# Gated linear layer: the scores' diagonal as elementwise products of keys and queries, summed over the features on TensorE by a column of ones

## What is computed

```
b = cumsum(g);  decay[t,s,d] = exp(b[t,d] - b[s,d]) for s <= t, else 0
A[t,s] = sum_d q[t,d] * k[s,d] * decay[t,s,d]
o[t]   = sum_s A[t,s] * v[s]  +  (q[t] * exp(b[t])) @ S
S      = exp(b_last) * S + sum_s k[s] * exp(b_last - b[s]) * v[s]^T
```

## Time and profile before

| | us |
|---|---|
| median of 3 runs | 1822.11 (1821.92 to 1822.14) |
| the profiled execution's own time | 1821.95 |
| its span, first to last instruction | 1820.2 |
| TensorE (PE) busy | 1803.8, 99% |
| weight loads (PEld) busy | 1518.1, 83% |
| VectorE (DVE) busy | 1270.2, 70% |
| ScalarE (ACT) busy | 942.4, 52% |
| HBM traffic | 179 GB/s mean |

### The profile page before, as it was taken

How to read it: one execution, slowest core, us unless ns; L and a number is a source line. 1 busy time by engine, 2 the same in 40 slices (tenths; PEclk the granted TensorE clock), 3 DMA queues, 4 the chain that set the end, 5 groups by cost and what they waited for, 6 DMA issues and landing times.

```text
span 1820.2 us, 24366 instructions
## 1 busy us (share of the span) xinstructions
PE 1803.8 (99%) x8863; PEld 1518.1 (83%) x8863; DVE 1270.2 (70%) x1720; ACT 942.4 (52%) x1310; POOL 37.8 (2%) x116
## 2 busy tenths in 40 slices
PE   8999999999999999999999999999999999999999
PEld 7899998778888888887888888888878888888887
DVE  6766766588556755767887878787777556577764
ACT  4555554455465545636554545454445444565542
POOL 2000000000000004000000000000000000000000
PEclk9999999999999999999999999999999999999999
DMA  8555454668789887575554555544767776555443
GB/s 294 173 175 151 138 174 152 204 182 188 179 153 214 178 178 167 197 240 153 177 174 152 168 173 153 181 151 158 226 181 235 211 219 208 161 162 162 160 166 114
DMA packets 175067, 326.72 MB, mean 179 GB/s; under 512 B 16824, under 2 KB 24912, under 8 KB 174208
## 3 DMA queue, kind: packets, MB, share of 16 engines
q1 hardware_dynamic: 173840, 321.04, 61.2%
q10 hardware_dynamic: 576, 4.19, 0.6%
q0 software_dynamic: 560, 0.26, 0.1%
HBM read 319.68 MB, written 5.77 MB: 179 GB/s over the span
## 4 chain that ended last, share of the span: by engine, by line
PE 96%; DVE 2%; ACT 1%; issue 1%; DMA 0%; DVEq 0%
PE acc L388 27%; PE acc L390 27%; PE acc L389 27%; PE ps L650 2%; PE ps L2889 2%; PE ps L498 1%; PE acc L355 1%; PE acc L354 1%; PE acc L353 1%; ACT wsp L304 1%; PE ps L683 1%; DVE wsp L324 1%; PE acc L371 0%; PE acc L377 0%; PE acc L375 0%
## 5 line engine op out<-in xcount | busy, mean ns | idle before, releaser
L324 DVE TENSOR_TENSOR wsp<-wraw,wsp 128x1024 fp32r<-128x1024 f32 x576 | 696.3, 1224 | 333.1 <-ACT wsp L304 330.5
L304 ACT ACTIVATE wsp<-wraw 128x1024 fp32r<-128x1024 f32 x576 | 597.3, 1053 | 361.4 <-PE acc L390 329.1
L388 PE MATMUL acc<-wsp,ta 128*128 128x512 f32 x1664 | 660.3, 397 | 6.0 <-DVE wsp L324 3.8
L390 PE MATMUL acc<-wsp,ta 128*128 128x512 f32 x1664 | 649.8, 391 | 0.0
L389 PE MATMUL acc<-wsp,ta 128*128 128x512 f32 x1664 | 648.4, 390 | 0.0
L388 PEld LDWEIGHTS acc<-wsp,ta 128*128 128x128 f32 x1664 | 312.8, 188 | 72.9 <-issue 4.9
L390 PEld LDWEIGHTS acc<-wsp,ta 128*128 128x128 f32 x1664 | 312.4, 188 | 66.6
L389 PEld LDWEIGHTS acc<-wsp,ta 128*128 128x128 f32 x1664 | 313.0, 188 | 62.0
L388 PE MATMUL acc<-wsp,tb_hi 128*128 128x512 f32 x576 | 228.4, 397 | 0.0
L390 PE MATMUL acc<-wsp,tb_lo 128*128 128x512 f32 x576 | 225.1, 391 | 0.0
L389 PE MATMUL acc<-wsp,tb_hi 128*128 128x512 f32 x576 | 224.6, 390 | 0.0
(11 more groups left out here) (332 smaller groups left out, 1584.8 us busy)
## 6 DMA issues: line engine op xcount, KB each, us to landing
wraw<-in_ml_w_in SPq DMA_DIRECT2D x129, 512.0 KB, 5.9
wraw<-in_a_w_in SPq DMA_DIRECT2D x128, 512.0 KB, 3.8
wraw<-in_kv_w SPq DMA_DIRECT2D x64, 512.0 KB, 3.9
wraw<-in_b_w_in SPq DMA_DIRECT2D x64, 512.0 KB, 4.4
wraw<-in_mla_w_in SPq DMA_DIRECT2D x49, 512.0 KB, 4.5
wraw<-in_mla_w_out SPq DMA_DIRECT2D x32, 512.0 KB, 4.0
wraw<-in_ml_w_out SPq DMA_DIRECT2D x32, 512.0 KB, 4.4
wraw<-in_a_w_out SPq DMA_DIRECT2D x32, 512.0 KB, 3.9
```

The lines of the kernel that those rows point to most:

```text
L304: nc.scalar.activation(unit_of(whi, n, SPLIT, w), unit_of(wraw, n, RAW, w), ACT.Copy).then_inc(w_high, 1)
L324: nc.vector.tensor_tensor(unit_of(wlo, n, SPLIT, w), unit_of(wraw, n, RAW, w), unit_of(whi, n, SPLIT, w).bitcast(F32), ALU.subtract).then_ ...
L388: nc.tensor.matmul(o, xh, wh, start=first, stop=False)
L390: m = nc.tensor.matmul(o, xl, wh, start=False, stop=end)
```

## The change

On VectorE, the masking of the 8 whole squares leaves step 24. In its place `diag` does `scale(0)` at once, and then two elementwise products of all keys by all queries, [128 features x 512] each, into room 1 of `kx` and of `qx`; `distance(2)` follows. On TensorE, `diag` moves from after unit 21 to after unit 22 and waits for those two products. It has again 8 fp32 matmuls, with a 128 x 128 block of products as the stationary operand and one column of ones as the moving one, so that 8 columns of PSUM bank 0 get the sums over features. VectorE then makes `aT` at step 25, as the identity times the sum of each row, in one instruction over [128 x 1024].

```diff
-        L2_AT = {"turn": 16, "decay": 17, "diag": 21, "level": [23, 25, 27, 29, 31, 33, 35, 37], "gate": 38, "pv": 39,
+        L2_AT = {"turn": 16, "decay": 17, "diag": 21, "sums": 22, "level": [23, 25, 27, 29, 31, 33, 35, 37], "gate": 38, "pv": 39,
...
                     distance(0)
                     distance(1)
-                    dve.wait_ge(l2["dg"], 1 + g)
-                    nc.vector.tensor_tensor(aT, ps2(0).rearrange("p (n t) -> p n t", t=P),
-                                            ident[:].unsqueeze(1).to_broadcast([P, 8,
-                                                                                P]), ALU.mult).then_inc(l2["at"], 1)
                     scale(0)
+                    for half, room in enumerate((kx, qx)):
+                        n = slice(half * 2 * T, (half + 1) * 2 * T)
+                        nc.vector.tensor_tensor(room[:, 1, :], flat(kT2)[:, n], flat(qT2)[:, n],
+                                                ALU.mult).then_inc(l2["dg"], 1)
                     distance(2)
+
+                def diagonal():
+
+                    dve.wait_ge(l2["dg"], 3 + 3 * g)
+                    nc.vector.tensor_tensor(aT, ident[:].unsqueeze(1).to_broadcast([P, 8, P]),
+                                            ps[:, 0, 0:8].unsqueeze(2).to_broadcast([P, 8, P]), ALU.mult).then_inc(l2["at"], 1)
...
                 if u == L2_AT["diag"] + LAG:
                     diag()
+                if u == L2_AT["sums"] + LAG:
+                    diagonal()
...
                 def diag():
-                    pe.wait_ge(l2["qT"], 1 + g)
-                    pe.wait_ge(l2["kt"], 1 + g)
+                    pe.wait_ge(l2["dg"], 2 + 3 * g)
                     for n in range(8):
-                        m = nc.tensor.matmul(ps2(0)[:, n * P:(n + 1) * P], kT2[:, n, :], qT2[:, n, :], start=True,
-                                             stop=True)
+                        products_of = (kx, qx)[n // 4][:, 1, n % 4 * P:(n % 4 + 1) * P]
+                        m = nc.tensor.matmul(ps[:, 0, n:n + 1], products_of, ones[:, 0:1], start=True, stop=True)
                     m.then_inc(l2["dg"], 1)
...
-                if u == L2_AT["diag"]:
+                if u == L2_AT["sums"]:
                     diag()
```

## The result

The changed kernel takes 1845.74 us (median of 4 runs, 1844.88 to 1846.59) against 1822.11 before: 1.0129 times as long, 95% interval 1.0117 to 1.0141, some 23.6 us more. The forecast was 1835.2 with a range of 1830 to 1842: right in the sign, but the time lies 3.7 us above the range. The profiled execution took 1844.88, with a span of 1843.2, 23.0 more than before.

What follows compares the result with a forecast made beforehand. The prediction took the length of TensorE's queue (busy 99% of the span) as the bound: block gain nothing, waits 4 x 3.3 = 13.2 us, all else nothing, added to 1821.95 gives 1835.1, stated as 1835.2; range 1830.0 to 1842.0.

Steps and rivals of the forecast that it cites:

- TensorE's block itself: TensorE's 16 records per group: paced by weight loads, 16 x 0.107 = 1.71 us as before, a gain of nothing.
- When the products are there: TensorE after unit 22: waits from 900.63 until VectorE's second product ends at 903.8, some 3.2 us per group.
- the sum of 4 x 3.3: Unit 23 on TensorE starts 3.3 us later, start-up included, in each of four groups: 13.2 us.
- What else moves: Other work on VectorE, ScalarE, DMA queues and later TensorE steps: no further wait, nothing given back, 0 us.
- none felt: Rival, TensorE behind unit 22: VectorE has the products by the time TensorE comes; 1822, or 1819 with cheap records; chance 0.03.
- a second one: Rival: products come later than added up, by a further ScalarE wait or late level 1; 4.5 us more, 1839.7; chance 0.04.
- The pause slows TensorE down: Rival, TensorE behind each pause: a slow stretch costing 1.8 us more each, 7.3 in all, 1842.5; chance 0.22.

Runs made afterwards that it cites:

- e1: The changed kernel with the two products moved to the head of VectorE's step 24, ahead of the first distance; 1822.15 us, ratio 0.9999.
- e2: The kernel before the change, with the moving operand of the diagonal's 8 products cut from 128 columns to 1; 1822.10 us, ratio 0.9999.
- e7: e1 with the products rounded to fp32r and two rounded columns of ones, one weight load per matmul instead of two; 1820.78 us, ratio 0.9992.
- e5: The changed kernel with the two products placed between distance(1) and scale(0), so that TensorE's pause is shorter; 1835.42 us, ratio 1.0074.
- e6: The changed kernel with TensorE's block one unit later, after unit 23 instead of 22; 1825.22 us, ratio 1.0018.
- e3: The changed kernel with 7 filling matmuls (identity by 256 columns of ones) on TensorE ahead of its wait for the products; 1837.15 us, ratio 1.0083.
- e4: The changed kernel with the old 128-column block in the new place, behind the wait for the two products, computed but not used; 1842.10 us, ratio 1.0107.

## Why the prediction was wrong, point by point

- *TensorE's block itself, a gain of nothing*: right. 1.70 us in e1 and e2 against 1.71. The rule of the Trainium skill that I had set beside it ("TensorE: Matmul & The Clock Gate", section "Back-to-back issue gap": about 25 ns between the starts of small matmuls) is no price for a stream in which every small matmul brings 128 columns of weights of its own: 0.107 us per record. The same section says that this figure leaves the weight loads out, which the prediction did not pass on. The same page's section "LDWEIGHTS (loading the stationary operand)" gives the columns divided by 1.2 in ns, 107 for 128, and the traces agree: 0.107 us per record here, 0.101 in e7.
- *When the products are there, the sum of 4 x 3.3*: right in place, cause and size. Products ending at 903.85, the block at 903.90, unit 23 at 905.73 (forecast 903.8, 903.9, 905.7); the wait's part of the loss is 12.8 us against 13.2. e1 shows that the whole loss hangs on it.
- *What else moves, at nothing*: right. No later wait appeared in the changed kernel; TensorE's waits for VectorE's splits are 3.2 us in all, beside 3.8 in the earlier trace rows. Neither of the rivals on the wait, none felt or a second one, came true. The spare time at level 5 is small, though, as e7 shows: 0.9 us in the kernel before.
- *The step that failed* is the sum's silent term, the rate of TensorE behind the pause, which I took as unchanged, and the chance of 0.22 that I gave to the rival "The pause slows TensorE down". What the runs show in its place is half clock in all four groups, 10.2 us of loss that the sum put at nothing. I had rows on either side of it (half pace behind 5.94 us of idle; the earlier trace rows: full pace behind 1.12), and leaned to the full clock since nothing lay between. In e5 the clock fell behind 1.7 us of idle time in three groups of four, in e6 behind 0.4 us in half of the executions, each time with the one-column block behind the pause. The earlier trace rows were a weak witness: the granted clock reads 1.00 in that stretch, so that no row shows what made the start of the kernel slow, while the slow stretches here do have a granted clock of 0.50.
- *The size of that rival* was low too: 1.8 us per pause, 7.3 in all, against 10.2. I took one stay at half clock per pause; here it comes in portions of 1.7 us of loss, and two of the four pauses brought two. With the measured size the sum comes to 1835.1 + 10.2 = 1845.3, beside the profiled execution's 1844.88. And the range ended at 1842.0, below the rival's own 1842.5, so that it left the rival out even as it was sized. The Trainium skill's rule on pauses (same page, section "HAM oscillation") pointed the right way, and the trace agrees: granted clock 0.50 behind each pause. It tells of longer pauses than those of e5 and e6, where the clock fell as well, behind 1.7 and 0.4 us.

What stays open: why the second portion follows in groups 1 and 3 and not in 0 and 2, why every run of e3 lost one or two portions where e1 and e2, with one-column blocks and no idle time either, lost none in any of their ten runs. The filling matmuls of e3 are themselves products of the identity and ones; whether that matters was not tried.

## What to carry to other kernels

Cutting the columns of a matmul saves nothing once the load of its weights is the longer part; look at the distance of the weight loads before counting columns, and save loads instead, for instance by a number type that needs one load per matmul. When a step is moved on to the product of another engine, put the time at which that product exists against the time at which the waiting engine comes by, and order the producer's instructions by who waits for them: here two instructions moved up by four places undid 23.6 us. And do not price a pause of TensorE at its length alone. Here pauses of 3.1 us with the one-column block behind them cost one or two portions of 1.7 us more each, those of 1.7 us one portion three times in four, and four of 0.4 us together 1.3 us more in half of the executions. Look at the mean granted clock of every run, and at short stretches behind each new pause.

## What was unexpected of the hardware

- The half clock comes in portions: every fall that the profiles show cost about 1.7 us or 3.4 us, 14 portions in all: 6 in the changed kernel, 1 in e3, 4 in e4 and 3 in e5; the profiles of e1, e2 and e6 have none. The spread of the run times follows it: 1844.9 and 1846.6 in the changed kernel, 1834.6 and 1836.2 in e5, and 1824.6 and 1826.0 in e6, the last with mean clocks of 1.000 and 0.999.
- A pause of 1.7 us (e5), and at times one of 0.4 us (e6), was followed by the half clock where the work behind was one column per weight load, although the profile's page counts TensorE as busy in that block (x16, 1.95 us). Where matmuls of 512 columns came behind it, a wait of 1.12 us was followed by the full pace.
- The profile page's clock line, in 40 slices, showed none of this; the mean clock of the run (0.994) and short stretches did.
